# Gated delta rule in a two-layer model kernel: one inverse for all five chunks, then a short state chain, in place of five full rounds

## What is computed

```
def gated_delta_rule(q, k, v, log_g, beta):
    ...
    gc = jnp.cumsum(log_g.reshape(B_, H, nc, CHUNK), axis=-1)
    decay = jnp.exp(jnp.where(causal, gc[..., :, None] - gc[..., None, :], -jnp.inf))
    kb = k * beta[..., None]
    lower = jnp.where(strict, jnp.einsum('bhnid,bhnjd->bhnij', kb, k) * decay, 0.0)
    rhs = jnp.concatenate([v * beta[..., None], kb * egc], axis=-1)
    sol = lax.linalg.triangular_solve(lower, rhs, left_side=True, lower=True, unit_diagonal=True)
    u_base, w = sol[..., :Dv], sol[..., Dv:]
    attn = jnp.where(causal, jnp.einsum('bhnid,bhnjd->bhnij', q, k) * decay, 0.0)
    ...
    def step(S, inp):
        u_b, w_c, a_c, qd, kd, dl = inp
        u = u_b - jnp.einsum('bhck,bhkv->bhcv', w_c, S)
        o = jnp.einsum('bhck,bhkv->bhcv', qd, S) + jnp.einsum('bhij,bhjv->bhiv', a_c, u)
        S = S * dl[..., None, None] + jnp.einsum('bhck,bhcv->bhkv', kd, u)
        return S, o
```

## Time and profile before

| | |
|---|---|
| median of three runs | 4125.67 us (4125.08 to 4134.72) |
| the profiled execution | 4139.84 us |
| its span | 4138.1 us |
| busy over the span: TensorE, VectorE, ScalarE, GpSimd | 84%, 41%, 17%, 15% |
| mean granted clock of TensorE | 0.905 |

### The profile page before, as it was taken

The page is one execution under the profiler, slowest core; times in us unless marked ns, Lnnn a source line. Parts: engine busy times, 40 slices in busy tenths (PEclk is TensorE's granted clock), DMA queues, the critical chain, the costliest instruction groups (busy, mean ns, idle before and its releaser), DMA issues. The chain is left out here.

```text
span 4138.1 us, 48435 instructions
## 1 busy us (share of the span) xinstructions
PE 3482.5 (84%) x16676; PEld 2455.7 (59%) x16676; DVE 1704.2 (41%) x4271; ACT 697.8 (17%) x1515; POOL 605.8 (15%) x516
## 2 busy tenths in 40 slices
PE   8998768999989477998998688888779977788886
PEld 7875646887866476787786434333357764333433
DVE  2113333111122643211124576677512336676774
ACT  1001121101001111110122122222111311222221
POOL 0000000000000000000000244444300004444442
PEclk9998557999999788999998899999999998999999
DMA  4441002443422000343332599999842328999995
GB/s 169 147 151 71 0 0 76 145 156 122 151 108 99 2 3 2 122 154 132 136 130 100 237 421 421 421 422 422 357 156 83 131 92 355 421 422 421 422 421 207
DMA packets 113651, 828.17 MB, mean 200 GB/s; under 512 B 12528, under 2 KB 14064, under 8 KB 15120
## 3 DMA queue, kind: packets, MB, share of 16 engines
q0 software_dynamic: 73728, 536.90, 31.2%
q1 hardware_dynamic: 37184, 273.59, 18.0%
q10 hardware_dynamic: 2576, 15.59, 1.0%
HBM read 824.99 MB, written 1.05 MB: 200 GB/s over the span
## 5 line engine op out<-in xcount | busy, mean ns | idle before, releaser
L2090 PE MATMUL psum_all<-expert_rows,const_sb 128*128 128x512 f32 x2048 | 988.3, 641 | 265.0 <-ACT const_sb L2036 263.4
L1881 POOL DMA_INDIRECT expert_rows<-in_peer_uv_dram,head_experts x512 | 605.6, 1183 | 3463.5 <-issue 2434.3
L2090 PEld LDWEIGHTS psum_all<-expert_rows,const_sb 128*128 128x128 f32 x2048 | 409.9, 204 | 826.2 <-issue 488.4
L1971 DVE CUSTOM_DVE_ANT_0 expert_rows<-expert_rows,xn 128x1024 f32<-128x1024 f32 x512 | 618.5, 1224 | 312.2 <-DMA expert_rows<-in_peer_uv_dram,head_experts 307.1
L261 PE MATMUL psum_all<-xn,weight_ring 128*128 128x272 f32 (+1 forms) x3200 | 732.3, 392 | 0.0
L261 PEld LDWEIGHTS psum_all<-xn,weight_ring 128*128 128x128 f32 x3200 | 613.4, 192 | 118.8
L261 PE MATMUL psum_all<-hidden,weight_ring 128*128 128x272 f32 (+1 forms) x1408 | 318.6, 389 | 0.0
L261 PEld LDWEIGHTS psum_all<-hidden,weight_ring 128*128 128x128 f32 x1408 | 267.5, 190 | 50.5
L1599 PE MATMUL psum_all<-x,weight_ring 128*128 128x256 f32 x1024 | 229.0, 382 | 0.0
L2036 ACT ACTIVATE const_sb<-cst,head_weights 128x128 f32<-128x128 f32 x512 | 163.7, 390 | 321.4 <-DVE head_weights L1977 318.3
L1599 PEld LDWEIGHTS psum_all<-x,weight_ring 128*128 128x128 f32 x1024 | 192.9, 191 | 28.6 <-issue 2.9
(11 more groups left out here) (480 smaller groups left out, 3333.2 us busy)
## 6 DMA issues: line engine op xcount, KB each, us to landing
weight_ring<-in_ffn_in_dram SPq DMA_DIRECT2D x88, 1024.0 KB, 4.8
weight_ring<-in_w_in_dram SPq DMA_DIRECT2D x48, 1024.0 KB, 5.0
weight_ring<-in_ffn_out_dram SPq DMA_DIRECT2D x32, 1408.0 KB, 6.0
weight_ring<-in_peer_q_dram SPq DMA_DIRECT2D x16, 1024.0 KB, 7.9
weight_ring<-in_hyb_in_dram SPq DMA_DIRECT2D x12, 1024.0 KB, 4.8
wv<-in_w_v_dram ACTq DMA_DIRECT2D x8, 1024.0 KB, 7.7
weight_ring<-in_br_attn_dram SPq DMA_DIRECT2D x8, 1024.0 KB, 5.9
weight_ring<-in_br_lru_dram SPq DMA_DIRECT2D x8, 1024.0 KB, 6.5
```

What stands on the lines that cost most here:

```text
L1881: pool.indirect_dma_start(out=rows[:, j, :], out_offset=None, in_=a["peer_uv"], in_offset=bass.IndirectOffsetOnAxis(ap=idx[:, n, j:j + 1], ...
L1971: dve.tensor_tensor_reduce(row, row, xt[:, n, :], 1.0, 0.0, ALU.mult, ALU.add, dots[:, n, j:j + 1]).then_inc(S.dotted, 1)
L2090: mm = pe.matmul(sums(n, half), diag[:, j, :], rows[:, j, D + half * 512:D + (half + 1) * 512], start=False, stop=last and j == TOPK - 1)
```

## The change

The five rounds are taken apart. Everything that does not need the state is done for all five chunks at once, straight from the full tensors: 10 blocks (5 chunks of 2 groups) of 64 columns.

- The chunk copies are gone. One negation of `cum` is left in their place.
- TensorE: 40 decay products, 20 key products, then the turning of kd and v (36 products against the identity, in five groups `turns`), with the 20 query products before the last group.
- VectorE: minimum, NT and the masks on 512 + 128 or 640 columns; the `strict` mask is gone, since the level masks already hold it. The causal mask and the product of the attention scores (`attention`) stand after the level masks and before the first copy of X. ScalarE takes the exponential and the copies out of PSUM.
- The inverse runs once, with 320 columns per stream. Its six masked copies `NL` lie in the idle region of the weight ring, as `sqo` of the next phase now does.
- The state chain follows, written out per chunk: R (not for the first), U, then S before O, with two state buffers. The O copies into `og` move from VectorE to ScalarE. The first chunk has no R and no product with the state, the last has no S.

The core of the diff:

```diff
-    def solve_dve(dve, S, step, c, groups, b, banks_of):
+    def solve_dve(dve, S, step, c, groups, b, banks_of, beside=None):
...
         for l in range(1, LEVELS):
             last = level(l)
+        if beside is not None:
+            beside()
...
+                    BLOCKS = NC * GDN_H // 2
+                    MAIN = 8
...
+                    sb_ = solver_buffers(c4, BLOCKS, "gdn", xn[:, :, :].rearrange("p k t -> p (k t)"), w.ring[:, (g % 2) * REGION:(g % 2 + 1) * REGION])
...
-                                for dst, src in copies:
-                                    dve.tensor_copy(dst[:, :, :], src[:, :, bass.ts(c, C)])
...
+                            dve.tensor_scalar(rneg[ROW_A:64, :], cum[ROW_A:64, :], -1.0, None, ALU.mult).then_inc(S.negated, 1)
+                            dve.wait_ge(S.decay_scores, 1)
+                            dve.tensor_scalar(dmat[:, MAIN_COLS], score_main(DECAY), 0.0, None, ALU.min).then_inc(S.decays, 1)
+                            dve.tensor_scalar(dmat[:, LAST_COLS], score_last(DECAY), 0.0, None, ALU.min).then_inc(S.decays, 1)
...
+                            def attention():
+
+                                step(dve.tensor_tensor(blocks3(dmat[:, :]), blocks3(dmat[:, :]), const("incl").unsqueeze(1).to_broadcast([P, BLOCKS, C]), ALU.mult))
+                                dve.wait_ge(S.scores, 2)
+                                dve.wait_ge(S.turned_in, len(turns))
...
+                            solve_dve(dve, S, step, 0, BLOCKS, sb_, solver_banks, attention)
+
+                            for c in range(NC):
+                                if c:
+                                    dve.wait_ge(S.r_product, c)
+                                    dve.tensor_tensor(R[:, :, :], vt[:, 2 * c:2 * c + 2, :], psum[2][:, 0:2 * P].rearrange("p (g n) -> p g n", g=2),
+                                                      ALU.subtract).then_inc(S.r_ready, 1)
...
-                            with pe.Fori(0, NC) as c:
-                                pe.wait_ge(S.chunk_in, c + 1)
...
+                            products(KEYS, kb)
+                            for n, (_, src, first, count, bank) in enumerate(turns):
+                                if n == 3:
+                                    pe.wait_ge(S.decays, 2)
+                                if n == 4:
+                                    products(QUERIES, gq)
...
+                            pe.wait_ge(S.turned_in, len(turns) - 1)
+                            solve_pe(pe, S, 0, BLOCKS, sb_, solver_banks)
+                            hold(pe, S, (S.xt_ready, LEVELS * STREAMS), (S.attn_ready, 2))
+                            for c in range(NC):
+                                before = state[:, c % 2, :, :]
+                                if c:
+                                    pe.wait_ge(S.state_ready, c)
...
-                        sqo = c5.enter_context(nc.sbuf_tensor("sq_o", [P, GDN_H, T], F32))
+                        sqo = w.slot(g % 2, 0, GDN_H * T).rearrange("p (h t) -> p h t", h=GDN_H)
```

More of the change, by code:

```diff
@@ L674, in hybrid @@
+                    solver_banks = [[psum[n][:, 0:BLOCKS * C // STREAMS] for n in stream] for stream in ((4, 5, 1), (6, 7, 0))]
                     heads = [(h, h // 2, slice((h % 2) * C, (h % 2) * C + C)) for h in range(GDN_H)]
-                    with phase(nc, *SOLVE, "chunk_in", "scores", "decays", "d_exp", "turned", "turned_in", "r_product", "r_ready",
-                               "u_product", "u_ready", "o_product", "o_read", "s_product", "dve_held") as (block, S):
+                    tokens = lambda c: slice(c * C, (c + 1) * C)
@@ new lines, in hybrid @@
+                    score_last = lambda kind: last_bank(kind)[:, 0:2 * C]
+                    turns = ((kdt, kd, 0, 4, psum[5][:, :]), (kdt, kd, 4, 4, psum[6][:, :]), (vt, gv, 0, 4, psum[7][:, :]), (vt, gv, 4, 4, psum[0][:, :]),
+                             (vt, gv, 8, 2, psum[3][:, 2 * C:2 * C + 2 * P]))
+                    out_banks = lambda c: (6, 7) if c % 2 else (0, 1)
+                    with phase(nc, *SOLVE, "negated", "decay_scores", "scores", "decays", "d_exp", "turned", "turned_in", "attn_ready", "r_product", "r_ready",
+                               "u_product", "u_ready", "o_product", "o_read", "s_product", "state_ready") as (block, S):
@@ L690, in take_in_late @@
[L690 to L734, removed]
+                            blocks3 = lambda t: t.rearrange("p (b i) -> p b i", i=C)
+                            dve.tensor_scalar(rneg[ROW_A:64, :], cum[ROW_A:64, :], -1.0, None, ALU.mult).then_inc(S.negated, 1)
@@ new lines, in _, with products @@
+                                    pe.matmul(o, sel, cum[ROW_A:64, tokens(c)], start=True, stop=False)
+                                    mm = pe.matmul(o, rneg[ROW_A:64, tokens(c)], sel, start=False, stop=True)
+                            mm.then_inc(S.decay_scores, 1)
+                            def products(kind, right):
+                                for c in range(NC):
+                                    for h, g_, q in heads:
+                                        mm = pe.matmul(score_block(kind, 2 * c + g_)[q, :], gk[:, h, tokens(c)], right[:, h, tokens(c)], start=True, stop=True)
+                                mm.then_inc(S.scores, 1)
@@ new lines, in _ @@
+                            products(KEYS, kb)
[4 more added lines that the diff above has]
+                                    products(QUERIES, gq)
+                                for b in range(count):
+                                    for h in ((first + b) % 2 * 2, (first + b) % 2 * 2 + 1):
+                                        q = slice((h % 2) * C, (h % 2) * C + C)
+                                        mm = pe.matmul(bank[q, b * P:(b + 1) * P], src[:, h, tokens((first + b) // 2)], ident, start=True, stop=True)
+                                mm.then_inc(S.turned, 1)
@@ L771, in _ @@
                                 mm.then_inc(S.u_product, 1)
                                 pe.wait_ge(S.u_ready, c + 1)
+                                if c < NC - 1:
+                                    for h, g_, q in heads:
+                                        mm = pe.matmul(psum[(4, 5)[h % 2]][:, g_ * P:(g_ + 1) * P], kdt[q, 2 * c + g_, :], U[q, g_, :], start=True, stop=True)
+                                    mm.then_inc(S.s_product, 1)
+                                if c >= 2:
+                                    pe.wait_ge(S.o_read, c - 1)
```

106 lines of the change are left out of this document (59 added, 47 removed).

## The result

The changed kernel takes **4021.54 us**, the median of four runs (4018.51 to 4025.29). The kernel before took 4130.19 us in four runs beside it (4125.08 to 4142.48). The ratio is 0.9733, with a 95% interval of 0.9708 to 0.9758. The forecast was 4054 us with a range of 4038 to 4074: faster was right, but the size was wrong, and the range did not hold the time. The gain is 108.6 us where 72 were forecast.

What follows compares the result with a forecast made beforehand. No engine is full: the 149.2 us stage is one waiting chain run five times. Inverse end 457.3 + chain 39.6 + code 2 = 498.9 against 571.0, 72 us less; 4125.67 - 72 = 4054 us, range 4038 to 4074.

Steps and rivals of the forecast that it cites:

- Start and decays: Stage head: one negation replaces memset and copies, first decay product at 422.4; 40 decay products take 4.3 us, until 426.7.
- the nearer row: Decay products: 0.107 us each, from the RWKV stage's order on 64x64 tiles, so 4.3 us; the other end was 12.4.
- VectorE leads until 438.0: Between decays and inverse: VectorE's minimum, masks and attention products take 11.3 us with hand-overs; TensorE is ready at 436.6 and waits.
- The clock: TensorE's clock rises some 5 us into the dense products before the inverse, then falls in the chain's first chunk or two.
- rival C: Whole stage: the clock does not rise; inverse 31 us, end at 514, 57 us less, 4069 us; chance 0.16.
- Rival B: State chain: the clock holds throughout, 24.6 us instead of 41.6, 15 us below the forecast, 4039 us; chance 0.13.
- The chain, 39.6 us: State chain over five chunks: 41.6 us at 1.2 GHz, less 2 us for the clock falling only after the start.
- Code that is no longer a loop, 2 us: TensorE's five rounds become straight code, about 980 products' records; 2 us added for fetching instructions.
- Rival D: Straight code from first score to last O: TensorE runs out of code, needing 6.6 us per fetched piece; slower, chance 0.01.
- E: In the stage: one more dependency, decays at 12.4 us and levels of 6 us, 8 + 10 us less gain, 4072; chance 0.08.
- Nothing else in the program may change: Phases before and after the stage: held at nothing, since they wait at a barrier and no weight transfer waits on it.
- a change behind the barrier as a sign that it was wrong: Outside the stage: any change before 421 us or after the barrier, held at nothing by the sum, would show the forecast wrong.

Runs made afterwards that it cites:

- the mixing run: The changed kernel with each head's key product put ahead of its two decay products, so 128-row and 32-row products alternate again; 4039.16 us.
- the second profile of the change: The changed kernel, unaltered, run again on one chip beside the version with extra products in the chain's gaps; 4020.0 us, ratio 0.9712.
- the run with 30 hidden instructions: The kernel before plus 30 empty TensorE semaphore increments in the phase ahead of the RWKV loop, where TensorE waits anyway; 4086.97 us, ratio 0.9867.
- the run with 140: The kernel before plus 140 empty semaphore increments on TensorE in the output norm of the gated rule, ahead of the RWKV loop; 4115.04 us.
- 59: The kernel before plus 59 empty semaphore increments on TensorE in the output norm of the gated rule; 4092.9 us, ratio 0.9909.

## Why the prediction was wrong in size

Step by step, as the prediction put it:

- *Start and decays.* The first product was forecast for 422.4 and came at 423.01. The 4.3 us of the decays measured 4.5, and the mixing run shows that the nearer row was the right one to take. Of the two reasons given, the one that carries is the other form of product ahead; the change of halves is worth 0.9 us.
- *VectorE leads until 438.0, the inverse at 438.1.* The attention products end on VectorE at 438.05, in part by luck: VectorE began 0.8 us later than said, when the decays ended at 427.52, and took 10.5 us where 11.3 was said. The first product behind it was forecast for 438.1 and comes at 438.60, and one level takes 3.86 us where 3.9 was said. The inverse ended at 457.76, forecast 457.3.
- *The clock.* It rose within the turning products, as assumed, and rival C is out. It fell in chunk 1; only chunk 0 and a part of chunk 1 ran at 1.00. The moment is not fixed: in the second profile of the change the clock was at 0.98 in 425 to 429 us, at 0.50 again in 436 to 438 us, and at 1.00 from 439 to 462. Rival B did not happen, and even with the gaps filled the clock held only to chunk 3.
- *The chain, 39.6 us.* Measured 497.01 - 457.76 = 39.3. The order of S and O gives 1.1 us a chunk of the 1.4 that were said of it.
- *Code that is no longer a loop, 2 us.* Measured nothing. The stage fetches nine pieces, and among TensorE's waits in it there is none for "issue". The Trainium skill's page Runtime: NRT & Kernel Launch, Instruction fetch mechanics, says straight code is fetched ahead; here it is. Rival D has no ground, and neither has E.
- Together the stage gave 74.8 us, where the sum said 72; 2 of the 2.8 are the code term.

**The step that failed is the first sentence of the sum: "Nothing else in the program may change".** The reason given was a barrier and the weight transfers. Both hold for data, and neither holds for the place of code. The loop in the RWKV mixer lies 1595 instructions further on, its code then stays in TensorE, and 46.5 us of the profile's 121.4 are won there; the run with 30 hidden instructions gives 53.9 us (0.9847 to 0.9888) for the same cause. The prediction did name a change behind the barrier as a sign that it was wrong, and that is the sign that came.

The rows for it stood in the prediction. The RWKV stage fetched 11 pieces in 51 us where the loop being rewritten fetched two in 160 (the 51 us are a round and part of the next; a round has eight or nine), and TensorE stood 1.34 us in mid-code. I used these as a price per piece for the new straight code. They were instead the sign of a loop that does not stay, and of a cost that any change ahead of it can switch on or off. The same page of the Trainium skill names a taken branch to code outside the fetched window as the stall; I tried this rule on the short loop alone, found that it turns in 0.22 us, and let it go. But a round of that loop is some 440 instructions, fewer than two pieces of 256 hold, so it was hardly a test of the rule. On the long loop the trace agrees with it: "issue" for 5.4 us at the loop's head. The page's window of two pages does not agree: a loop of 1700 instructions turns without a single packet when it lies well. That fits the size that the same section of the page gives for TensorE alone, 128 KiB or 2048 instructions.

What is not settled: the threshold lies between 0 and 30 instructions, but why a bad place costs 47 us in one case and 12 or 21 in others, and why one round of the run with 140 nearly stayed, was not found. Nor were the places between 59 and 140 tried. That the loop stays in seven pieces and not in eight is argued: all places tried agree with it if the loop of the kernel before starts 226 to 255 instructions into a piece of 256 (an estimate from the runs and the 1700 instructions), but no run shows where a piece begins.

## What to carry to other kernels

Before you hold a part of the program at nothing, look at the packets of the instruction queue in each long loop behind the edit. A loop that fetches in every round is paying, and whatever lengthens or shortens the code ahead of it may remove or bring that cost. To measure a change by itself, put the loop back in its place with empty instructions in a wait, or try the kernel before with them: a gain that appears there is not the change's. Sort products of one tile kind into runs, and where a chain alternates with short waits, see whether the wait is costing the clock as well.

## What the runs showed that I had not expected

- A loop of about 1700 TensorE instructions runs with no code fetched from its second round on, at 37.2 us a round. With 30 instructions fewer ahead of it, it fetches eight or nine pieces of 16 KB in every round and takes 47 to 50 us from the second on. The granted clock is 0.83 to 0.89 in those rounds, and about half of the loss is put down to it.
- An empty semaphore increment on TensorE takes 0.15 us, so 128 of them are worth hiding.
- Products that change their kind from one to the next take some 0.17 us a record at clock 0.50, against 0.053 in runs of one kind.
- More work made the chain shorter: with 16 more small products a chunk took 5.9 to 6.0 us instead of 9.40, as long as the clock stayed.
